# First feed-forward product of a two-layer block: high and low parts of the tokens moved as one operand of 512 columns, halves added from PSUM

## The reference, cut to what matters

```python
h = rmsnorm(x, norm_ffn[l])                      # [256, 1024]
u = jnp.square(jax.nn.relu(h @ w_ff1[l]))        # [256, 4096]
x = x + u @ w_ff2[l]                             # [256, 1024]
```

## Time and profile before

| | |
|---|---|
| median of 3 runs | 1125.55 us (1125.32 to 1125.84) |
| the profiled execution | 1124.9 us |
| its span, first to last instruction | 1123.1 us |
| mean granted TensorE clock | 0.985 |
| PE / PEld / DVE / ACT busy | 1088.3 / 952.4 / 710.7 / 626.6 us |

### The profile page before, as it was taken

How to read it: one execution, slowest core, us unless ns; L and a number is a source line. 1 busy time by engine, 2 the same in 40 slices (tenths; PEclk the granted TensorE clock), 3 DMA queues, 4 the chain that set the end, 5 groups by cost and what they waited for, 6 DMA issues and landing times.

```text
span 1123.1 us, 17492 instructions
## 1 busy us (share of the span) xinstructions
PE 1088.3 (97%) x6848; PEld 952.4 (85%) x6848; DVE 710.7 (63%) x1203; ACT 626.6 (56%) x993; POOL 60.9 (5%) x80
## 2 busy tenths in 40 slices
PE   8999999999999999999999999999999899999997
PEld 6897889998888987789989987898988678989885
DVE  4799686556557888685555565684455656844555
ACT  4665745445445756654544454856556447565562
POOL 1010100000000100100000000004000000040000
PEclk8999999999999999999999999999999899999999
DMA  8862346555666543256556546554444446544431
GB/s 279 244 193 79 110 146 205 192 181 178 195 189 206 182 132 113 95 186 188 189 181 192 189 152 188 187 151 135 129 132 139 142 132 187 151 128 130 138 132 57
DMA packets 89087, 181.17 MB, mean 161 GB/s; under 512 B 8797, under 2 KB 19933, under 8 KB 89005
## 3 DMA queue, kind: packets, MB, share of 16 engines
q1 hardware_dynamic: 87565, 175.79, 50.3%
q10 hardware_dynamic: 1440, 4.26, 1.2%
HBM read 178.98 MB, written 1.05 MB: 160 GB/s over the span
## 4 chain that ended last, share of the span: by engine, by line
PE 80%; DVE 9%; ACT 5%; issue 4%; DMA 2%; POOL 0%; SPq 0%; POOLq 0%; DVEq 0%; ACTq 0%
PE bank L784 23%; PE bank L786 23%; PE bank L785 23%; DVE w_lo L1655 3%; ACT w_hi L1266 2%; DMA raw<-in_w_in 2%; PE bank L861 2%; PE bank L912 2%; PE bank L959 1%; DVE xn L1906 1%; PE bank L968 1%; PE bank L969 1%; PE bank L1202 1%; PE bank L967 1%; PE bank L935 1%
## 5 line engine op out<-in xcount | busy, mean ns | idle before, releaser
L1655 DVE TENSOR_TENSOR w_lo<-raw,w_hi 128x1024 fp32r<-128x1024 f32 (+1 forms) x320 | 389.4, 1220 | 301.2 <-ACT w_hi L1266 296.6
L1266 ACT ACTIVATE w_hi<-raw 128x1024 fp32r<-128x1024 f32 (+1 forms) x320 | 334.5, 1051 | 232.6 <-PE bank L786 211.3
L784 PE MATMUL bank<-h_hi,w_hi 128*128 128x256 f32 x896 | 257.4, 287 | 0.0
L786 PE MATMUL bank<-h_hi,w_lo 128*128 128x256 f32 x896 | 253.4, 283 | 0.0
L785 PE MATMUL bank<-h_lo,w_hi 128*128 128x256 f32 x896 | 253.3, 283 | 0.0
L784 PE MATMUL bank<-w_hi,h_hi 128*128 128x512 f32 (+1 forms) x448 | 182.7, 408 | 5.4 <-DVE h_lo L1674 4.8
L785 PE MATMUL bank<-w_lo,h_hi 128*128 128x512 f32 (+1 forms) x448 | 176.3, 393 | 0.0
L786 PE MATMUL bank<-w_hi,h_lo 128*128 128x512 f32 (+1 forms) x448 | 176.1, 393 | 0.0
L784 PEld LDWEIGHTS bank<-h_hi,w_hi 128*128 128x128 f32 x896 | 170.9, 191 | 3.9 <-issue 3.5
L785 PEld LDWEIGHTS bank<-h_lo,w_hi 128*128 128x128 f32 x896 | 171.0, 191 | 0.5
L786 PEld LDWEIGHTS bank<-h_hi,w_lo 128*128 128x128 f32 x896 | 170.9, 191 | 0.0
(11 more groups left out here) (290 smaller groups left out, 1297.8 us busy)
## 6 DMA issues: line engine op xcount, KB each, us to landing
raw<-in_w_in SPq DMA_DIRECT2D x144, 512.0 KB, 3.8
raw<-in_w_ff SPq DMA_DIRECT2D x128, 512.0 KB, 3.9
raw<-in_w_out SPq DMA_DIRECT2D x40, 512.0 KB, 3.2
raw<-in_w_in SPq DMA_DIRECT2D x8, 404.0 KB, 6.2
xn<-in_cmp_w SPq DMA_DIRECT2D x8, 256.0 KB, 5.1
x_sb<-in_x SPq DMA_DIRECT2D x2, 512.0 KB, 7.5
mix<-in_cmp_w SPq DMA_DIRECT2D x4, 256.0 KB, 4.5
gain<-in_cmp_w SPq DMA_DIRECT2D x4, 256.0 KB, 5.0
```

Of the source, the lines that this page charges most:

```text
L784: pe.matmul(out_ap, s_hi, m_hi, start=start, stop=False, **kw)
L786: return pe.matmul(out_ap, s_lo, m_hi, start=False, stop=stop, **kw)
L1266: act.activation(slot(w_hi, u), slot(raw, u), ACT.Copy).then_inc(hi_ready, 1)
L1655: dve.tensor_tensor(slot(w_lo, u), slot(raw, u), slot(w_hi, u).bitcast(F32), ALU.subtract)\
```

## The change

For ff1 alone, `h_hi` and `h_lo` become two halves of one tensor `h_parts`, and a new `hidden_unit` issues two matmuls where there were three: the high weights against both parts at once (512 columns, in two runs of 256), and the low weights against the high part (256 columns). The high x high and high x low products lie in the two halves of one bank, so each feature group c needs a bank of its own. A tile fills the four banks 4 to 7, and every tile uses the same four. DVE adds the halves with a `tensor_reduce` per bank and takes relu and square in one instruction (`scalar_tensor_tensor`), ACT copies the result into `u_hi`, DVE subtracts as before. The transposes of quarter (1,1) of the norms ahead of ff1 go to bank 0. Nothing is loaded that was not loaded before.

```diff
--- before.py
+++ after.py
@@ -63,6 +63,7 @@
 DVE_TURNED = 9
 FEATURE1 = (0, 1)
 FEATURE2 = (4, 5, 8, 9)
+FFN_NORMS = [2 * l + 1 for l in range(L)]
 LAM_INIT = [0.8 - 0.6 * float(np.exp(-0.3 * l)) for l in range(L)]
 
 
@@ -138,7 +139,7 @@
         steps.append(key)
 
     def norm_turn(n, i, u):
-        use(("norm", n, i, u), 4 + 2 * u + i)
+        use(("norm", n, i, u), 0 if n in FFN_NORMS and i and u else 4 + 2 * u + i)
         step("norm", n, i, u)
 
     def order_in_norm(n, i, u):
@@ -351,17 +352,17 @@
         tail(("out", 0, l), w_out[l], (1, 2, 3), 2 * l + 1, (0, 2, 1, 3))
 
         def ff1(t):
-            for i in range(2):
-                use(("ff1", l, t, i), 4 + 2 * (t % 2) + i)
+            for c in range(4):
+                use(("ff1", l, t, c), 4 + c)
             for q in range(4):
                 if t == 0 and q == 1:
                     norm_turn(2 * l + 1, 1, 1)
                 if t == 0 and q == 2:
                     step("stats", 2 * l + 1)
                 src = w_ff1[l][256 * q:256 * q + 256, 512 * t:512 * t + 512].rearrange("(k p) c -> p k c", p=P)
-                unit(("ff1", l, t, q), src, closes=("ff1", l, t, 1) if q == 3 else None)
-            for i in range(2):
-                done(("ff1", l, t, i))
+                unit(("ff1", l, t, q), src, closes=("ff1", l, t, 3) if q == 3 else None)
+            for c in range(4):
+                done(("ff1", l, t, c))
             step("square", l, t)
 
         def ff2(t):
@@ -469,8 +470,8 @@
         raw = sb("raw", [P, SLOTS, UNIT])
         w_hi = sb("w_hi", [P, SLOTS, UNIT], F32R)
         w_lo = sb("w_lo", [P, SLOTS, UNIT], F32R)
-        h_hi = sb("h_hi", [P, KD, T], F32R)
-        h_lo = sb("h_lo", [P, KD, T], F32R)
+        h_parts = sb("h_parts", [P, 2, KD, T], F32R)
+        h_hi, h_lo = h_parts[:, 0, :, :], h_parts[:, 1, :, :]
         const = sb("const", [P, C_END])
         sel = sb("sel", [STACK, 8 * P], F32R)
         masks = sb("masks", [P, 2 * P], BF16)
@@ -570,7 +571,7 @@
         u_hi = [exact(f"u_hi{b}", arena_at, 2048 * b, 4, T) for b in range(2)]
         u_lo = [exact(f"u_lo{b}", arena_at, 2048 * b + 1024, 4, T) for b in range(2)]
         u_full = part(4096, 2, 512)
-        relu = part(5120, 2, 512)
+        u_sum = part(5120, 4, T)
 
         mixT1_hi = [exact(f"mixT1_hi{g}", arena_at, lo, 4, T) for g, lo in enumerate((2856, 0))]
         mixT1_lo = [exact(f"mixT1_lo{g}", arena_at, lo, 4, T) for g, lo in enumerate((3880, 1440))]
@@ -627,7 +628,7 @@
         h_ms_ready, m_ms_ready, m_rstd_ready = sem("h_ms_ready"), sem("m_ms_ready"), sem("m_rstd_ready")
         diff_weights, diff_mixed = sem("diff_weights"), sem("diff_mixed")
         nsa_mixed, mlstm_mixed, fox_mixed = sem("nsa_mixed"), sem("mlstm_mixed"), sem("fox_mixed")
-        u_hi_ready, u_ready = sem("u_hi_ready"), sem("u_ready")
+        u_squared, u_hi_ready, u_ready = sem("u_squared"), sem("u_hi_ready"), sem("u_ready")
         sel_ready = sem("sel_ready")
         lam_dots, lam_exp = sem("lam_dots"), sem("lam_exp")
         stick_log = sem("stick_log")
@@ -830,6 +831,25 @@
                                            skip_group_check=True)
                     if q == 3 and c == 1:
                         close(mm, uses_of[0])
+                finish_unit(mm, key)
+
+            def hidden_unit(key, uses_of, q, there):
+
+
+                hi, lo = weights(key)
+                for c in range(4):
+                    ps = open_bank(uses_of[c]) if q == 0 else bank[bank_of[uses_of[c]]]
+                    for kk in range(2):
+                        k = 2 * q + kk
+                        if there and k % 4 == 0 and c == 0:
+                            there(0, k)
+                            there(1, k)
+                        f = slice(c * P, (c + 1) * P)
+                        pe.matmul(ps[:, :].rearrange("p (a t) -> p a t", a=2), hi[:, kk, f], h_parts[:, :, k, :], start=k == 0,
+                                  stop=False, skip_group_check=True)
+                        mm = pe.matmul(ps[:, 0:T], lo[:, kk, f], h_hi[:, k, :], start=False, stop=k == KD - 1, skip_group_check=True)
+                    if q == 3 and c < 3:
+                        close(mm, uses_of[c])
                 finish_unit(mm, key)
 
             def out_unit_products(key, name, hi_f, lo_f, first, last=False, accs=range(4)):
@@ -1151,7 +1171,7 @@
                     elif kind == "ff1":
                         _, _, t, q = s
                         there = features_there(n0 + 1) if t == 0 else None
-                        feature_unit(s, [("ff1", l, t, i) for i in range(2)], q, there)
+                        hidden_unit(s, [("ff1", l, t, c) for c in range(4)], q, there)
                     elif kind == "ff2":
                         f = s[3]
                         if f % 2 == 0:
@@ -1448,16 +1468,11 @@
                         turned(s, mixT1_hi[g][:, c:c + 2, :])
                     elif kind == "square":
                         t = s[2]
+                        split_to(at_unit[("ff1", l, t, 3)] + AHEAD - 1)
                         for i in range(2):
-                            n = 16 * l + 2 * t + i
-                            ps = src(("ff1", l, t, i))
-
-                            if n >= 2:
-                                act.wait_ge(u_ready, n - 1)
-                            free(act.activation(relu[:, i, :], ps[:, :], ACT.Relu), ("ff1", l, t, i))
-
-                            act.activation(u_hi[t % 2][:, 2 * i:2 * i + 2, :], relu[:, i, :].rearrange("p (c t) -> p c t", c=2),
-                                           ACT.Square).then_inc(u_hi_ready, 1)
+                            act.wait_ge(u_squared, 16 * l + 2 * t + i + 1)
+                            act.activation(u_hi[t % 2][:, 2 * i:2 * i + 2, :], u_full[:, i, :].rearrange("p (c t) -> p c t", c=2),
+                                           ACT.Copy).then_inc(u_hi_ready, 1)
 
 
             for l in range(L):
@@ -2005,11 +2020,14 @@
                     elif kind == "square":
                         t = s[2]
                         for i in range(2):
+                            for c in (2 * i, 2 * i + 1):
+                                key = ("ff1", l, t, c)
+                                ps = src(key)
+                                free(dve.tensor_reduce(u_sum[:, c, :], ps[:, :].rearrange("p (a t) -> p t a", a=2), AX.X, ALU.add), key)
+                            r = u_sum[:, 2 * i:2 * i + 2, :].rearrange("p c t -> p (c t)")
+                            dve.scalar_tensor_tensor(u_full[:, i, :], r, 0.0, r, ALU.max, ALU.mult).then_inc(u_squared, 1)
+                        for i in range(2):
                             n = 16 * l + 2 * t + i
-                            split_to(at_unit[("ff1", l, t, i)] + AHEAD - 1)
-                            drained(dve, ("ff1", l, t, i))
-                            r = relu[:, i, :]
-                            tt(u_full[:, i, :], r, r, ALU.mult)
                             dve.wait_ge(u_hi_ready, n + 1)
                             b = slice(2 * i, 2 * i + 2)
                             dve.tensor_tensor(u_lo[t % 2][:, b, :], u_full[:, i, :].rearrange("p (c t) -> p c t", c=2),
```

## The result

| | before | changed |
|---|---|---|
| median of 5 runs | 1125.55 us (1124.15 to 1127.09) | 1130.69 us (1129.65 to 1132.90) |
| ratio, 95% interval | | 1.0047 (1.0035 to 1.0058) |
| profiled execution, its span | 1124.9, 1123.1 us | 1132.9, 1131.1 us |
| mean granted clock of the profiled execution | 0.985 | 0.981 |

A forecast was written before the change was run, and what follows sets the result against it. PE was taken to bound the kernel. Against the profiled 1124.9 us, -5.5 (saving) + 4.5 (Wait A) + 2.7 (Wait B) = +1.7 gave 1126.6; the runs' median being 0.65 higher, 1127.2 us, range 1124.8 to 1130.8.

The forecast's parts named there:

- The saving: PE's ff1 units: 8 fewer matmuls in each of 64 units, each saving a fixed 10.8 ns, 5.5 us in all.
- The rival of no saving: ff1 matmuls: the operand in two runs costs as two matmuls while the waits remain; 1132.7 us, chance 0.05.
- The rival of the load-bound step: ff1: weight loads set the 256-column step, so pairing saves 5.5 us more; 1121.7 us, chance 0.10.
- Wait A: Unit 0 of ff1(0): PE waits for bank 6 until DVE's `h_lo` frees it; 2.23 us a layer, 4.5 in all.
- Wait B: Start of ff1(1): PE waits for DVE's reduces to free ff1(0)'s banks; 1.37 us a layer, 2.7 in all.
- dearer and cheaper rivals: DVE reduce at 0.95 us instead of 0.69: 1129.4 us, chance 0.12; the cheap reduce: 1125.6 us, chance 0.04.
- The clock falls in wait A: Rival: PE runs at half clock after the wait, 1.7 us per fall; 1128.9 or 1130.6 us, chance 0.27.
- Cover: Later tiles: DVE's split of the fourth unit ahead is done 1.1 us before PE wants it, so no wait.

The follow-up runs named there:

- e5: Changed kernel with norm quarter (0,1) moved to bank 2 and DVE's four reduces of tile 0 put ahead of its weight split; 1121.77 us, ratio 0.9973.
- e6: Changed kernel with both waits removed, and high and low part laid side by side so the 512 columns are one run; 1121.82 us, ratio 0.9975.
- e7: The changed kernel measured again with no edit; 1130.08 us, ratio 1.0049.
- e4: Kernel before the change, with only a PE wait for norm quarter (0,1) added ahead of group 2 of ff1(0)'s unit 0; 1130.56 us, ratio 1.0050.
- e1: Changed kernel with norm quarter (0,1) moved to bank 2, which takes Wait A away; 1125.05 us, ratio 0.9992.
- e3: Changed kernel with eleven unread 512-column matmuls issued on PE in the place of Wait A; 1128.86 us, ratio 1.0023.
- e8: Changed kernel with every DVE reduce done twice, output the same; one execution, 1158.66 us.
- e9: Changed kernel with both waits removed, and each feature group's two 512-column matmuls issued before its two 256-column ones; 1121.95 us, ratio 0.9971.
- e2: Changed kernel with DVE's four reduces of tile 0 put ahead of its weight split and squares, taking Wait B away; 1129.15 us, ratio 1.0032.

## Why the prediction was right or wrong

**The saving.** 5.5 us forecast; e5's stages give 5.2. The fixed part of about 10 ns is there. The rival of no saving falls by e5, and e6 shows that the distance of the two runs costs nothing. The rival of the load-bound step falls too: it would have made an ff1 tile of 32 pairs 10.8 us (0.2292 and 0.109 us a pair), and none came under 11.09. The 2.5 ns a matmul of the Trainium skill ("TensorE: Matmul & The Clock Gate", Back-to-back issue gap) give an estimate of 1.3 us in all; e5's 5.2 do not agree with it. What the rows of before could not show are the two kinds of tile; with the long kind throughout, as in layer 0 of e7, the stage saves 0.7 us less.

**Wait A.** 2.23 us a layer forecast, 2.15 in e4 and 2.2 in e1: right in place, releaser and size.

**Wait B.** 1.37 us a layer forecast; e1 and e5 differ in it alone, 175.59 against 174.32: 1.27. The square was mis-sized by 0.06 us. The price of the reduce, 0.69, was right, and its dearer and cheaper rivals fall.

**The step that failed: "The clock falls in wait A ... Chance 0.27."** The forecast's sum leaves the clock at 1.00. With the clock held there, by e3, the stage is 0.87 us longer than before, which is the sum; with it free, it fell behind 7 of 10 waits and cost 1.3 to 1.5 us each. The reason I gave against it, that PE is dense ahead of wait A while it was idle for long ahead of the fall in the earlier trace rows, does not hold: in the changed kernel's profile PE is busy for all of the 3.40 us from 160.50 to 163.90, and the clock fell all the same, as it did behind most of the waits A. The fall was in the text, as a rival with 1128.9 for one fall and 1130.6 for two. Its weight was wrong, its price (1.7 against 1.46) a little high. That the medians of 1130.7 and 1130.1 meet its figure for two falls is partly luck: 7 of 10 waits at 1.4 us are 2.0 us a run and give 1129.2, and the medians carry 0.9 to 1.5 us more that these two stages do not explain.

**Cover.** "The cover is 1.1 us" held, and a little more: no wait in later tiles as it stands, and about 1.6 us paid in each with 2.9 us of DVE added (e8), so 1.3.

Left over: the stages of a profile and the medians do not meet closely. For the changed kernel the medians say +5.1 and +4.6 and the stages +4.7 and +4.1; but for e1 it is -0.9 against -2.7, for e3 +2.9 against +1.7, for e5 -3.7 against -5.2, for e9 -2.9 against -5.4, for e4 +4.6 against +5.8. The part between the stages (e5) accounts for some of it; the rest stays open. The costs of the waits and of the fall rest on the stages, their signs on both.

## What to carry to other kernels

A saving of ten nanoseconds on each of hundreds of instructions is safe only where no bank changes its neighbours: list for each bank the user before, which engine frees it, and what stands ahead of that in the engine's queue. A stop of PE like this one, 2.4 us, can cost more than its length; reckon with the half clock behind it, and if the stop can't be moved, try to fill it. Two small edits, a bank number and four reduces put ahead of a split, turned a loss of 0.47% into a gain of 0.27%.

## What the runs showed of the hardware that was not expected

The same wait of 2.39 us was followed by the half clock in one layer of one execution and not in the other (e4). With eleven products without use in its place it stayed at 1.00 in both layers of one execution (e3). Pairs of a 512- and a 256-column matmul ran at two paces, 11.10 and 11.29 us for 32 pairs: tile by tile in turn in most layers, all six later tiles at the slower one in one layer each of e2, e7 and e8. Two long then two short ones ran at a single pace, 11.15 (e9). A reduce of 512 elements in two halves out of PSUM took 0.69 us, on the line through 422 ns for 256 elements read and 1221 for 1024, so by the elements read and not by the 256 written.
